# Three stand-alone norms: DVE adds the chunks' squares, TensorE sums two rows over the partitions in place of eight

## The reference, cut to what matters

```python
def rms_norm(x, w):
    xf = x.astype(jnp.float32)
    y = xf * lax.rsqrt(jnp.mean(xf * xf, axis=-1, keepdims=True) + EPS)
    return (y * w.astype(jnp.float32)).astype(x.dtype)
```

## Time and profile before

| what | value |
|---|---|
| median of 3 runs | 2549.89 us (2549.51 to 2555.36) |
| span of the profiled execution | 2549.0 us |
| PE busy | 2363.6 us (93%) |
| PEld busy | 1970.3 us (77%) |
| DVE busy | 1072.8 us (42%) |
| ACT busy | 791.1 us (31%) |
| chain that ended last, by engine | PE 87%, DVE 7%, ACT 3%, issue 2% |
| row sums of L1274 in the whole kernel | 144 records, 52.2 us busy, mean 521 ns |
| mean granted TensorE clock | 0.947 |

### The profile page before, as it was taken

One profiled execution on the slowest core, in us unless ns is written; L12 is line 12 of the kernel. 1 busy time (PEld: TensorE's weight loads), 2 busy tenths in 40 slices (PEclk: granted clock), 3 DMA queues, 4 the chain that ended last, 5 costly groups with the idle time before them and its releaser, 6 DMA issues.

```text
span 2549.0 us, 34929 instructions
## 1 busy us (share of the span) xinstructions
PE 2363.6 (93%) x13320; PEld 1970.3 (77%) x13320; DVE 1072.8 (42%) x1528; ACT 791.1 (31%) x1208; POOL 47.2 (2%) x75
## 2 busy tenths in 40 slices
PE   8999998999978998999998999999558997999997
PEld 7988975789944776888886744998458996989895
DVE  4442323333365345344344222333863335445445
ACT  3222113321265233232233244222214233323232
POOL 0000000000000000000000000000410000000000
PEclk9999999999987899999999879999888999999998
DMA  3333210333200322333332200332002321333333
GB/s 116 91 101 97 88 53 25 107 91 91 83 26 9 105 87 74 99 93 94 93 99 94 66 1 2 112 117 75 1 1 85 127 87 47 93 91 91 99 90 100
DMA packets 53737, 197.66 MB, mean 78 GB/s; under 512 B 6928, under 2 KB 7184, under 8 KB 53024
## 3 DMA queue, kind: packets, MB, share of 16 engines
q1 hardware_dynamic: 49248, 179.39, 23.2%
q10 hardware_dynamic: 3456, 14.02, 1.5%
q0 software_dynamic: 960, 3.24, 0.4%
HBM read 190.21 MB, written 6.42 MB: 77 GB/s over the span
## 4 chain that ended last, share of the span: by engine, by line
PE 87%; DVE 7%; ACT 3%; issue 2%; POOL 0%; DMA 0%; ACTq 0%; DVEq 0%; POOLq 0%
PE ps L1251 73%; PE ps L1274 2%; PE ps L1414 1%; PE ps L1453 1%; DVE tmp L1126 1%; PE ps L1475 1%; PE ps L1399 1%; PE ps L1499 1%; DVE hf L1119 1%; DVE xl L724 1%; PE ps L1354 1%; PE ps L1489 1%; PE ps L1339 1%; PE ps L1411 1%; PE ps L1300 0%
## 5 line engine op out<-in xcount | busy, mean ns | idle before, releaser
L1251 PE MATMUL ps<-xh,wh 128*128 128x264 f32 (+1 forms) x3040 | 789.5, 319 | 35.9 <-DVE xl L724 24.8
L1251 PE MATMUL ps<-xl,wh 128*128 128x264 f32 (+1 forms) x3040 | 782.5, 317 | 0.0
L1251 PE MATMUL ps<-xh,wl 128*128 128x264 f32 (+1 forms) x3040 | 780.7, 317 | 0.0
L1251 PEld LDWEIGHTS ps<-xh,wh 128*128 128x128 f32 x3040 | 507.6, 191 | 87.4 <-issue 29.2
L313 ACT ACTIVATE wh<-wraw 128x1024 fp32r<-128x1024 f32 x338 | 356.4, 1054 | 644.4 <-PE ps L1251 642.9
L714 DVE TENSOR_TENSOR wl<-wraw,wh 128x1024 fp32r<-128x1024 f32 x338 | 413.6, 1224 | 292.6 <-ACT wh L313 283.4
L1251 PEld LDWEIGHTS ps<-xl,wh 128*128 128x128 f32 x3040 | 504.9, 191 | 35.2 <-issue 0.8
L1251 PEld LDWEIGHTS ps<-xh,wl 128*128 128x128 f32 x3040 | 503.9, 191 | 35.4
L1251 PE MATMUL ps<-bh,wh 128*128 128x512 f32 (+1 forms) x816 | 284.5, 368 | 1.9 <-DVE wl L714 1.7
L1251 PE MATMUL ps<-bl,wh 128*128 128x512 f32 (+1 forms) x816 | 286.0, 370 | 0.0
L1251 PE MATMUL ps<-bh,wl 128*128 128x512 f32 (+1 forms) x816 | 284.5, 368 | 0.0
(11 more groups left out here) (243 smaller groups left out, 1727.6 us busy)
## 6 DMA issues: line engine op xcount, KB each, us to landing
wraw<-weights_dram SPq DMA_DIRECT2D x338, 512.0 KB, 3.5
hf<-tables_dram POOLq DMA_DIRECT2D x12, 264.0 KB, 3.0
res<-x_t_dram SPq DMA_DIRECT2D x4, 528.0 KB, 6.1
res<-x_t_dram ACTq DMA_DIRECT2D x1, 2112.0 KB, 8.3
res_dram<-res ACTq DMA_DIRECT2D x1, 2112.0 KB, 7.1
mrg_dram<-mrg ACTq DMA_DIRECT2D x1, 2112.0 KB, 8.4
mrg<-mrg_dram ACTq DMA_DIRECT2D x1, 2112.0 KB, 8.2
res<-res_dram ACTq DMA_DIRECT2D x1, 2112.0 KB, 8.6
```

What stands on the lines that cost most here:

```text
L1251: last = nc.tensor.matmul(o, w[:, slot, wchunk(c), :], a[:, c, tok], start=(c == chunks[0] and w is wh and a is hi), stop=(c == chunks[-1] ...
```

## The change

In the three stand-alone norms ACT writes the first square to `hf[:, 0]` and the others to `tmp` in turn, and from the fourth on a square waits for an addition (`sq_added`) and not for TensorE. `norm_apply` begins with six additions on DVE, squares 1 to 6 onto `hf[:, 0]`, by the helper `add_squares`, which was a local function before. TensorE calls `sum_added`, the tail of the old `strips_and_sums`, which waits for all additions and the eighth square and sums two rows. Norms at the end of a product keep their form (`squares=False` where `norm_apply` follows one). The counters `n_sq` on DVE now count the squares of these norms where they occur.

```diff
@@ def norm (ACT)
             def norm(src, n, wait=lambda c: None):
+                nonlocal n_sq, n_added
+                tok = slice(T - n, T)
                 for c in range(KC):
-                    sum_squares(src[:, c, T - n:T], lambda: wait(c))
+                    wait(c)
+                    if c == 0 and n_sq:
+                        act.wait_ge(sq_used, n_sq)
+                    if c >= 3:
+                        act.wait_ge(sq_added, n_added + c - 2)
+                    nc.scalar.activation(tmp[:, c % 2, tok] if c else hf[:, 0, tok], src[:, c, tok], ACT.Square)\
+                        .then_inc(sq_ready, 1)
+                n_sq += KC
+                n_added += KC - 2
                 act.wait_ge(sq_used, n_sq)
@@ DVE
+            def add_squares(c, tok):
+                dve.wait_ge(sq_ready, n_sq + c + 1)
+                if c > 1:
+                    dve.wait_ge(sq_added, n_added + c - 1)
+                nc.vector.tensor_tensor(hf[:, 0, tok], hf[:, 0, tok], tmp[:, c % 2, tok], ALU.add)\
+                    .then_inc(sq_added, 1)
+
+            def norm_apply(src, w, n, split_first=False, squares=True):
+
+                nonlocal n_hi, n_x, n_sq, n_added
+                if squares:
+                    for c in range(1, KC - 1):
+                        add_squares(c, slice(T - n, T))
+                    n_sq += KC
+                    n_added += KC - 2
                 root_made()
@@ TensorE
             def strips_and_sums(B, src, n, ready, chunks=range(KC)):
+                strips(B, KC, src, n, ready, chunks)
+                sum_added(n)
+
+            def sum_added(n):
 
                 nonlocal n_sq, n_added
-                strips(B, KC, src, n, ready, chunks)
                 n_sq += KC
                 n_added += KC - 2
                 pe.wait_ge(sq_added, n_added)
@@ at each of the three places
-            sum_rows(4, KC, T)
+            sum_added(T)
```

More of the change, by code:

```diff
@@ L729, in root_made @@
                 dve.wait_ge(root_ready, n_root)
-            def norm_apply(src, w, n, split_first=False):
-                nonlocal n_hi, n_x
+            def add_squares(c, tok):
[11 more added lines that the diff above has]
+                    n_added += KC - 2
                 root_made()
@@ L798, in summed_strips @@
                 tok = slice(T - n, T)
[L800 to L805, removed]
                 for c in range(KC):
@@ L811, in summed_strips @@
                     if c >= 2:
-                        add(c - 1)
+                        add_squares(c - 1, tok)
                 n_sq += KC
@@ L976, in add_to_res @@
                 return nc.vector.tensor_tensor(res[:, c, NM:T], src, res[:, c, NM:T], ALU.add)
-            n_sq += KC + 2 * RH
+            n_sq += 2 * RH
             summed_strips(START["w_out"], SEQ, add_to_res)
-            norm_apply(res, "norm2_w", SEQ)
+            norm_apply(res, "norm2_w", SEQ, squares=False)
             n_hf += KC
@@ L1168, in _ @@
             dve.wait_ge(x_ready, n_x)
-            n_sq += KC + 2 * GH
+            n_sq += 2 * GH
             summed_strips(START["w_o"], T, lambda c, src: nc.vector.tensor_copy(two(mrg[:, c, :]), src))
@@ L1221, in _ @@
                         ins.then_inc(evicted[p0[2]], 1)
-            n_sq += KC
             summed_strips(START[f"glu{g}down"], SEQ, lambda c, src: nc.vector.tensor_tensor(
```

## The result

The changed kernel is slower. Four runs gave a median of 2565.64 us (2561.30 to 2571.77) beside 2550.91 us for the four of the kernel before; the ratio is 1.0053 with a 95% interval of 1.0035 to 1.0071. Forecast were 2559.0 us (1.0036) within 2554.5 to 2562.5. The sign and the mechanism came out, the time lies 3.1 us above the range. The profiled execution is the shortest of the four, with a span of 2559.4 us, 10.4 more than the one of before.

The account below looks back on a forecast made before the run. TensorE's strip products were taken to bound the kernel (73% of the span), the norms mattering only as gaps; +2.40, +0.34 and +6.40 us gave +9.14 on span 2549.0, thus 2558.1, and 2559.0 us as median, range 2554.5 to 2562.5.

Parts of the forecast that it names:

- The sign and the mechanism: Three stand-alone norms: slower (chance 0.66), as six DVE additions (4.35 us per norm) and a slow two-row sum delay each logarithm.
- The sum's clock: Two-row sum in each norm: TensorE, idle some 10 us or more before, runs it slowly, 3.99 us; lower bound 2.09.
- The rival of the full clock: All three norms: TensorE sums two rows at 2.4 GHz, 2.09 us each, so only +3.4 us, 2553.3; chance 0.10.
- The gap between additions: DVE's six additions per norm: each starts 0.03 us after its predecessor ends, 0.73 us from start to start.
- the loop's 0.15: DVE's additions: gap of 0.15 us, seen for a dependent pair inside a counted loop, upper end 4.95 us per norm.
- The first norm: Additions from 9.84, after DVE's lambda work, to 14.19; logarithm at 18.24 against 15.84, +2.40 us.
- The second norm's: Additions 1358.50 to 1362.85, sum from 1362.91, logarithm at 1366.90 against 1366.56: +0.34 us.
- After the logarithm: Root, scaling, splits and strips behind each norm: all follows at the old distances, nothing added.
- the last line of the sum: Whole kernel: span 2558.1 plus the 0.9 by which the earlier median, 2549.89, exceeds its span gives 2559.0 us, +0.36%.
- TensorE's clock elsewhere: Stages behind the norms: granted clock shifts by chance, a few us; faster, 2542 or less, 0.04; part given back, 2556, 0.08.
- the range's upper end: Whole kernel: 2559.0 plus 3.3 us (loop's gaps 1.8, late clock 1.5), rounded to 2562.5.
- the norms' sum, +9.14: Three stand-alone norms together: +2.40, +0.34 and +6.40 us of later logarithms.

Follow-up runs that it names:

- e1: The changed kernel run again unaltered, against the kernel before: ratio 1.0040.
- e4: The changed kernel plus products of constants in TensorE's idle time ahead of each two-row sum, timed against the kernel before: ratio 1.0023.
- e5: The kernel before run again unaltered, for its own scatter and a second profile: ratio 0.9999.
- e7: The kernel before plus a delay of nine dependent DVE additions, results unread, behind the third norm's root: ratio 1.0027.
- e14: The kernel before plus delays of three, one and nine dependent DVE additions behind the roots of the three norms: ratio 1.0046.
- e13: The changed kernel timed a third time unaltered, against the kernel before: ratio 1.0052.

## Why the prediction was off, point by point

- **The mechanism was right.** Additions in DVE's own order behind the last update of the residual, then a two-row sum at the low clock, with the third norm as the largest part: 6.40 forecast, 6.75 measured, in all three profiles of the changed kernel.
- **The sum's clock** (3.99 us) was right: 3.89 to 3.91 in seven of the nine sums, 3.62 and 3.79 in e1's first and second norm. The rival of the full clock did not occur of itself; e4 made it, and it is worth 5.0 us, not 5.7, chiefly as the second norm's sum was only in part at the high level (2.53 us, the others 2.06).
- **The gap between additions** was mis-sized, 0.03 for 0.11 us: the earlier trace rows has a pair with one wait, and the additions carry two. That is 0.4 us per norm, and the loop's 0.15 that I kept as the upper end covered it.
- **The first norm** began its additions 0.77 us earlier than forecast, as the lambda load landed earlier; hence +1.83 to +2.38 over its three profiles for +2.40.
- **The second norm's** base was one execution in which the load of the meta tokens landed some 0.45 us later than in seven others; and the changed stretch was 0.49 us above the forecast, from the gaps and the late square. The mean change is 1.2 and not 0.34.
- **After the logarithm** all follows as it did up to the last norm: 388.5 us behind the third norm in place of 388.6. Only behind DVE's last instruction the changed kernel is 0.7 to 0.9 us longer, in all its profiles; the sum had nothing for it.
- **The step that failed** is the last line of the sum, "The median of the runs, 2549.89, stands 0.9 above that span; the same distance gives 2559.0", together with the nothing that it puts for all stages outside the norms. Two of the three runs, 2549.51 and 2549.89, were at the short end of the kernel's own scatter: over 114 runs of the kernel before in this study (without e5's 11) the median is 2553.1 us (2549.2 to 2559.2), and 11 of them are at 2549.89 or below. The 15 runs of the changed kernel have a median of 2566.6, 7.6 us above the forecast. Of these, 3.2 are the base (2553.1 for 2549.9), 1.6 the norms and the end of the kernel (10.7 for 9.14), and the remaining 2.8 lie in neither; their cause stays open. The base alone does not explain the first timing: there the four runs of before have 2550.91, only 1.0 us more than the forecast's base, and the median of the changed kernel is 14.7 us above theirs. The rival "TensorE's clock elsewhere" was held to be chance of a few us to either side, and the range's upper end had no room for it.
- **Luck.** That the norms' sum, +9.14, comes so near to the first profile's +9.58 is in part luck: measured less forecast, its terms are off by -0.40, +0.49 and +0.35. In the first, the lambda load landed some 0.7 us earlier than in the profile of before, which hid the wider gaps.

## What to carry to other kernels

Fewer rows for TensorE save nothing where its row sums lie under another engine's work; the additions that replace them stand in that other engine's program order, behind its last piece. Weaving (as the norms at the end of a product do) and standing alone are different cases. And a short sum after a long pause of TensorE costs nearly twice its time; products of constants into a free bank ahead of it (5, 11 and 18 in e4) bring that back, though here the kernel with them was still slower than the one before, by 1.0023. When a kernel's times scatter by more than the change, forecast from the spread of many runs and not from a few that may be at its short end.

## What the runs showed of the hardware

- An addition of 128x528 that waits for its predecessor starts 0.04 us after its end with one wait (e7) and 0.11 with two (changed kernel); in the trace the second wait is an entry of 0.02 us by itself.
- The two-row sum: 3.90 us at the 1.2 GHz level after pauses of 11.7 and 17.7 us, 2.05 us at 2.4 GHz in e4. In e7 the clock read 0.50 from 2146.2 to 2159.7 with TensorE idle from 2144.0 to 2154.5, and once more from 2166.6 to 2169.9, after a pause of 1.8 us; the stretch behind the root was 8.2 us longer for a delay of 6.65, in e14, with the same delay, 6.7.
- The granted clock in the attention stages differs from execution to execution of one kernel (e1 and the first profile of the changed kernel), and with it the span, by up to 8 us.
- The end of the kernel is 0.7 to 0.9 us longer in the four profiles in which a packet of the instruction queue falls into it (changed kernel, e1, e13, e4).
